# Six slots for expert rows in place of eight, and two more slots for raw weights

## What is computed

```python
def chunk(hc):
    q = (hc @ w_pq).reshape(PEER_CHUNK, PEER_HEADS, 2, PEER_DK_HALF)
    sc = jnp.einsum('thcd,chnd->thcn', q, sub_keys).astype(jnp.float32)
    vals, idx = lax.top_k(sc, PEER_TOPK)
    ...
    experts = jnp.take_along_axis(
    ...
    g = jax.nn.softmax(top_s, axis=-1)
    ue = peer_u[experts]
    ve = peer_v[experts]
    act = jax.nn.gelu(jnp.einsum('td,thkd->thk', hc, ue).astype(jnp.float32), approximate=False)
    return jnp.einsum('thk,thkd->td', (g * act).astype(ve.dtype), ve)
```

## Time and profile before

| what | us |
|---|---|
| median of 3 runs | 1669.24 (1666.39 to 1669.46) |
| the profiled execution | 1668.97 |
| its span | 1667.2 |
| TensorE, VectorE, ScalarE, GpSimd busy | 1503.3, 1122.0, 750.1, 280.2 |
| mean granted TensorE clock | 0.983 of full |

### The profile page before, as it was taken

The page is one execution under the profiler, slowest core; times in us unless marked ns, Lnnn a source line. Parts: engine busy times, 40 slices in busy tenths (PEclk is TensorE's granted clock), DMA queues, the critical chain, the costliest instruction groups (busy, mean ns, idle before and its releaser), DMA issues.

```text
span 1667.2 us, 19514 instructions
## 1 busy us (share of the span) xinstructions
PE 1503.3 (90%) x7240; PEld 1106.9 (66%) x7240; DVE 1122.0 (67%) x2043; ACT 750.1 (45%) x1393; POOL 280.2 (17%) x317
## 2 busy tenths in 40 slices
PE   7999999999688888788898777779999999899999
PEld 6899988988544444344453232248888879788887
DVE  6669656665877676777876866457576656857654
ACT  5544553344344443434543433335555337645532
POOL 0000000000233333334343334312000002000000
PEclk9999999999899999999999999999999999999999
DMA  6744444552799999999999999973455653135553
GB/s 238 266 177 174 156 152 159 195 172 81 286 422 421 420 422 420 421 421 421 414 406 421 410 422 418 421 290 104 170 182 180 199 177 133 51 118 191 195 187 117
DMA packets 71310, 443.07 MB, mean 266 GB/s; under 512 B 7047, under 2 KB 9359, under 8 KB 25776
## 3 DMA queue, kind: packets, MB, share of 16 engines
q0 software_dynamic: 36864, 268.45, 38.8%
q1 hardware_dynamic: 30624, 165.69, 28.7%
q10 hardware_dynamic: 3728, 7.70, 1.3%
HBM read 440.75 MB, written 2.63 MB: 266 GB/s over the span
## 4 chain that ended last, share of the span: by engine, by line
PE 62%; DMA 20%; DVE 12%; ACT 4%; issue 3%; POOL 0%; ACTq 0%; SPq 0%; DVEq 0%; POOLq 0%
DMA arena<-experts,xn 19%; PE banks L1295 18%; PE banks L1326 11%; PE banks L1698 10%; PE banks L1266 9%; PE banks L1331 6%; DVE arena L2293 3%; PE banks L1588 2%; DVE w_lo L1877 2%; PE banks L1424 1%; PE banks L1447 1%; ACT xn L973 1%; ACT xn L977 1%; PE banks L1373 1%; PE banks L1461 1%
## 5 line engine op out<-in xcount | busy, mean ns | idle before, releaser
L1698 PE MATMUL banks<-arena,xn 128*128 128x512 f32 x1024 | 492.7, 618 | 119.6 <-ACT xn L977 119.4
L1877 DVE TENSOR_TENSOR w_lo<-raw,w_hi 128x2048 fp32r<-128x2048 f32 x154 | 352.5, 2290 | 191.0 <-PE banks L1295 94.3
L2293 DVE CUSTOM_DVE_ANT_0 arena<-arena,banks 128x1024 f32<-128x1024 f32 x256 | 311.7, 1218 | 194.0 <-DMA arena<-experts,xn 193.7
L1698 PEld LDWEIGHTS banks<-arena,xn 128*128 128x128 f32 x1024 | 186.2, 195 | 353.1 <-ACT xn L977 184.6
L694 ACT ACTIVATE w_hi<-raw 128x2048 fp32r<-128x2048 f32 x154 | 295.1, 1917 | 255.6 <-PE banks L1295 114.8
L629 POOL DMA_INDIRECT arena<-experts,xn x256 | 247.4, 966 | 425.6 <-PE banks L1698 406.9
L1295 PE MATMUL banks<-w_hi,op 128*128 128x512 f32 x896 | 226.6, 392 | 0.8 <-DVE op L2450 0.8
L966 ACT ACTIVATE xn<-xn,stat 128x2 f32<-128x2 f32 x128 | 37.8, 295 | 379.4 <-DVE xn L2293 379.3
L1326 PE MATMUL banks<-op,w_hi 128*128 128x512 f32 x792 | 199.0, 392 | 0.0
L1295 PEld LDWEIGHTS banks<-w_hi,op 128*128 128x128 f32 x896 | 167.8, 188 | 36.5 <-DVE op L2450 1.3
L1326 PEld LDWEIGHTS banks<-op,w_hi 128*128 128x128 f32 x792 | 142.3, 189 | 26.3 <-issue 1.1
(11 more groups left out here) (254 smaller groups left out, 1363.7 us busy)
## 6 DMA issues: line engine op xcount, KB each, us to landing
raw<-wstream SPq DMA_DIRECT2D x154, 1024.0 KB, 5.1
arena<-experts,xn POOLq DMA_INDIRECT x256, 12.8
xn<-mem_in ACTq DMA_DIRECT2D x2, 1024.0 KB, 7.1
scratch<-scratch ACTq DMA_DIRECT2D x1, 1536.0 KB
x<-x_in SPq DMA_DIRECT2D x2, 512.0 KB, 4.9
arena<-scratch ACTq DMA_DIRECT2D x1, 1024.0 KB, 7.2
raw<-keys_in SPq DMA_DIRECT2D x1, 1024.0 KB, 5.2
raw<-mem_in SPq DMA_DIRECT2D x1, 1024.0 KB, 11.4
```

The costliest lines, as they stand in the source:

```text
L1698: mm = pe.matmul(sums[:, n, :], diag[:, s, :], rows[:, s, D + n * CW:D + (n + 1) * CW], start=(at == 0), stop=(at == PAIRS - 1), skip_grou ...
L1877: dve.tensor_tensor(w_lo[:, n % LO, :, :], raw[:, SLOT[n], :, :], w_hi[:, n % HI, :, :].bitcast(F32), ALU.subtract).then_inc(lo_ready, 1)
L2293: dve.tensor_tensor_reduce(u, u, token_rows[k // PAIRS][:, :, :], 1.0, 0.0, ALU.mult, ALU.add, dots[:, s:s + 1]).then_inc(dot_ready, 1)
```

## The change

`GSLOTS` goes from 8 to 6 and `EXTRA` = 2 is new. `rows` takes the first 6 x 2048 numbers of the arena per partition, and the 4096 behind them become `extra`, two raw slots (3 and 4) for weight halves. Between halves 60 and 71 `ring()` deals the halves out over four slots (two of raw, two extra) in place of two, so that a half waits for the low part of the one four before it. The first half in each extra slot waits for `merged_lo` to be 4 in its stead, since the arena's part is in use by the mixer until then. The wait ahead of half 73 still names the last gather, which now lies in another slot. `diag` keeps its 128 columns per slot, in a view that isn't cut by GSLOTS. Nothing that is computed changes.

```diff
--- before.py
+++ after.py
@@ -42,7 +42,8 @@
 RAW = 3
 HI = 3
 LO = 2
-GSLOTS = 8
+GSLOTS = 6
+EXTRA = 2
 AHEAD = 2
 EXP_AT = 12
 
@@ -93,13 +94,14 @@
 def ring():
 
     first, later = 2 * CHUNKS.index("pq"), 2 * CHUNKS.index("ina")
+    inside = [(SPARE + 1) % RAW, (SPARE + 2) % RAW] + list(range(RAW, RAW + EXTRA))
     slot, turn, before = [], [], []
-    uses, held = [0] * RAW, [None] * RAW
+    uses, held = [0] * (RAW + EXTRA), [None] * (RAW + EXTRA)
     for n in range(NHALF):
         if n == first:
             uses[SPARE] += 2
             held[SPARE] = None
-        s = n % RAW if n < first else (SPARE + 1 + (n - first) % 2) % RAW if n < later else (SPARE + n - later) % RAW
+        s = n % RAW if n < first else inside[(n - first) % len(inside)] if n < later else (SPARE + n - later) % RAW
         slot.append(s)
         turn.append(uses[s])
         before.append(held[s])
@@ -311,6 +313,11 @@
         sub_root = part(6400, S)[0:HEADS, :]
         sub_step = part(6656, S)[0:HEADS, :]
 
+        extra = part(2 * GSLOTS * D, EXTRA, KC, HW)
+
+        def slot_of(n):
+            return raw[:, SLOT[n], :, :] if SLOT[n] < RAW else extra[:, SLOT[n] - RAW, :, :]
+
         keys = raw[:, SPARE, :, :].rearrange("p a (b k) -> p (a b) k", b=2)
         rows = part(0, GSLOTS, 2 * D)
         score = part(16384, TB, 2 * PH, NKEYS)
@@ -362,7 +369,7 @@
         mem_sq, mem_root = spare[:, 0:4, :], spare[:, 4:8, :]
         memory_banks = 4, 5
 
-        diag = xn[:, 0, :].rearrange("p (s n) -> p s n", s=GSLOTS)
+        diag = xn[:, 0, :].rearrange("p (s n) -> p s n", n=P)
         expert = xn[:, 1, 0:256].rearrange("p (t n) -> p t n", t=TB).bitcast(I32)
         weight = xn[:, 1, 256:512].rearrange("p (t n) -> p t n", t=TB)
         dots = xn[:, 1, 784:792]
@@ -379,7 +386,7 @@
         banks = [bank_pairs[i // 2][:, i % 2, :] for i in range(8)]
 
 
-        raw_in = [sem(f"raw_in{i}") for i in range(RAW)]
+        raw_in = [sem(f"raw_in{i}") for i in range(RAW + EXTRA)]
         hi_ready = sem("hi_ready")
         lo_ready = sem("lo_ready")
         norm_hi = sem("norm_hi")
@@ -565,7 +572,7 @@
         @block.sync
         def _(sp):
             def load(n):
-                r, landed = raw[:, SLOT[n], :, :], raw_in[SLOT[n]]
+                r, landed = slot_of(n), raw_in[SLOT[n]]
                 if CHUNKS[n // 2] in WIDE:
                     at = n % 2 * 4 * HW
                     sp.dma_start(r.rearrange("p (b a) c -> p b (a c)", b=2),
@@ -588,12 +595,15 @@
                 if n == 2 * CHUNKS.index("mkvb"):
                     misc_emptied(sp, ("sc", PH - 1))
                     sp.dma_start(mem_rows, mem2_in.rearrange("(t p) d -> p t d", p=P)).then_inc(raw_in[SPARE], 16)
+                if SLOT[n] >= RAW and BEFORE[n] is None:
+                    sp.wait_ge(merged_lo, 4)
                 if BEFORE[n] is not None:
                     sp.wait_ge(lo_ready, BEFORE[n] + 1)
                 if n == 2 * CHUNKS.index("ina"):
                     point(sp, "kmem_b")
                 if n == 2 * CHUNKS.index("ina") + 1:
-                    sp.wait_ge(gathered[GSLOTS - 1], 16 * (TB * PAIRS // GSLOTS))
+                    last = TB * PAIRS - 1
+                    sp.wait_ge(gathered[last % GSLOTS], 16 * (last // GSLOTS + 1))
                 load(n)
 
             for j in range(4):
@@ -691,7 +701,7 @@
 
                     if n >= HI:
                         act.wait_ge(half_done, n - HI + 1)
-                    act.activation(w_hi[:, n % HI, :, :], raw[:, SLOT[n], :, :], ACT.Copy).then_inc(hi_ready, 1)
+                    act.activation(w_hi[:, n % HI, :, :], slot_of(n), ACT.Copy).then_inc(hi_ready, 1)
                 halves[0] = max(halves[0], upto)
 
             def product(key):
@@ -1874,7 +1884,7 @@
 
                     if n >= LO:
                         dve.wait_ge(half_done, n - LO + 1)
-                    dve.tensor_tensor(w_lo[:, n % LO, :, :], raw[:, SLOT[n], :, :],
+                    dve.tensor_tensor(w_lo[:, n % LO, :, :], slot_of(n),
                                       w_hi[:, n % HI, :, :].bitcast(F32), ALU.subtract).then_inc(lo_ready, 1)
                 halves[0] = max(halves[0], upto)
 
```

## The result

The changed kernel takes 1702.15 us (median, 1700.5 to 1706.83), the kernel before 1669.35 in the same measurement: a ratio of **1.0205 (95% interval 1.0193 to 1.0217), slower by some 33 us**. The forecast was 1671.0 with a range up to 1679.0. The profiled execution took 1706.83 us (span 1705.0, mean granted clock of TensorE 0.973), against 1668.97 before; it has the same number of instructions, and most lines of the code stand ten further down (L629 is L639 now, L1698 is L1708, L2293 is L2303).

A forecast was written before the change was run, and what follows sets the result against it. The saturated DMA in the expert stage was taken to bound the kernel. Two halves leaving it gave -4.96 us and five dry stretches with six slots +6.7, net +1.7: about 1671 us, range 1663.8 to 1679.

The forecast's parts named there:

- What bounds the kernel: Expert stage: the 16 DMA engines are saturated for about 667 us, each MB moved costing 2.48 us.
- Two halves leave the stage, -4.96 us: Loads of weight halves 64 and 65 move ahead of the full expert stage, gaining 2 x 2.48 us.
- Least latency 5.8 us: Gathers: shortest issue to landing, taken from the first one on an idle DMA; median was to fall to about 8.
- Rival A: Expert stage: six-slot gathers take longer than 5.8 us, so short stretches cost more; 1677.6 us at 7.0; chance 0.26.
- The fill, 1.7 us: Stretch 453 to 469 us, start of the gathers: six slots leave the DMA engines dry for 1.7 us.
- 469 to 791: Long stretch of the expert stage, in us: smallest issue to landing 11.1, so 0.3 us to spare and no cost.
- m - 4.96 - 5.8: Time to spare with six slots in a stretch whose smallest issue to landing is m; below zero, engines run dry.
- A spell costs its worst row, not the sum: Dry stretches of the expert stage: later rows are already shifted, so each is charged once; five summed to +6.7 us.
- 927 to 950, 2.8 us for the two reciprocals: Expert stage: two 3.35 us VectorE reciprocals hold up dots and slots, so a row lands 2.8 us late.
- The quiet cadence and the tail: Stage end: a pair of gathers every 4.97 us, and unchanged time behind the last landing.
- Rival C: Early halves held by a wait taken for met, or VectorE's gate counts: cost without gain, +6.7, 1675.7 us; chance 0.03.
- rival B: Dry spells in the expert stage are free because engines don't end together, so all 4.96 us stay: 1664; chance 0.18.

The follow-up runs named there:

- e6: Kernel before with eight slots, halves 62 and 63 landing early in row slots 6 and 7, and rows weighed one at a time: 1663.74 us, ratio 0.9968.
- e1: Kernel before with GSLOTS 6 in place of 8 and nothing else, no weights in the arena: 1704.5 us, ratio 1.0209.
- e4: Changed kernel, six slots, with ScalarE weighing each row alone in place of in pairs: 1669.32 us, ratio 1.0001.
- e8: Changed kernel with TensorE multiplying only the first 512 of 1024 value columns for most rows, the rest left out: 1679.0 us, ratio 1.0061.
- e7: Kernel before with five slots and rows weighed one at a time: 1708.0 us, ratio 1.0235.
- e15: Kernel before, eight slots, with ScalarE weighing four rows at once in place of two: 1730.38 us, ratio 1.0385.
- e14: Changed kernel with one eighth of low parts 64 to 71, 12 of 48 matmuls per product half and evenly spread gate dots together: 1686.4 us, ratio 1.0111.
- e9b: Changed kernel with VectorE making only one eighth of the low parts of halves 64 to 71, the rest left out: 1701.04 us, ratio 1.0196.
- e10b: Changed kernel with 12 of the 48 matmuls of each product half in the stage, the others left out: 1695.97 us, ratio 1.0166.
- e11: Changed kernel with VectorE's 16 gate dots of a turn spread evenly over its 22 top-16 steps: 1703.62 us, ratio 1.0195.
- e3: Kernel before with seven slots, the small columns beside the rows keeping rings of eight: 1672.66 us, ratio 1.0023.

## Why the prediction was wrong, point by point

- **What bounds the kernel: right for before.** It was the DMA at 421 GB/s, and e6, which moves two halves ahead of the stage and keeps 418 GB/s in it, is faster.
- **Two halves leave the stage, -4.96 us: right in place and time** (404.78 and 417.6; share 0.59 from 400 to 420), and worth it only while the queue is full. With six slots in pairs they bring nothing that can be told from zero: e1 without them takes 1704.5, the changed kernel 1702.15, and the intervals overlap.
- **Least latency 5.8 us: right** (5.4 to 5.6 measured), and so was the median of about 8 (8.1). Rival A's point of decision, 6.1, was not reached, and yet its side came true. By the Trainium skill (page "DMA: Bandwidth & Descriptors", section "Latency and other measured facts") the memory's access time goes from 0.2 us on average to 2 us at high load. The least issue to landing doesn't show it: with the DMA nearly full it was no longer than the 5.8 us of the lone first gather.
- **The fill, 1.7 us: too small.** 2.9 us by bytes from 450 to 460 and 1.0 more to 470 (380 GB/s for 422), as the rejected estimate of 2 to 4 had it.
- **469 to 791, "0.3 to spare. Nothing.": this is the step that failed.** 421 GB/s became 383 from 500 to 600 and 382 from 600 to 700 (100 x 38 / 421 = 9 us each), and 401 from 700 to 800 (5 us). Two errors made it nothing. First, m - 4.96 - 5.8 was read from a kernel in which the queue is full, where the landing time shows only how long the row queued; the least of it doesn't show how far a row can fall behind when, for want of a queue, TensorE idles, gets the lower clock and holds the row 1.8 us longer (3.78 against 1.98). Nor does it show that product turns at 2.67 us a row can't catch up with a DMA at 2.48. The sum over the slot's round, 1.8 us left over, would have told that one such row uses it up. That sum was at hand in the earlier trace rows.
- **"A spell costs its worst row, not the sum": wrong.** It holds where all that follows is shifted alike. But a hole in the issues comes back one round later as a hole in the releases (6.42 us ahead of row 16, 6.96 ahead of row 22), and is only closed by what is left over in a round. Between 450 and 1140 us the number of packets in progress falls below 14 for 0.3 us or more some 30 times (before: 7, those behind the stage's end included), not five times. Rival A had the sentence for it ("If that long stretch ran short each time that TensorE's steps with weights come between the rows it would be worse still") and no number.
- **927 to 950, 2.8 us for the two reciprocals: about right.** The line of the earlier trace rows is the read-out of a dot, 0.08 us; the reciprocal starts in the same moment, and the reading of 3.35 us is right:

```profile
925.51 3.35 DVE L2322 RECIPROCAL raw<-raw 128x512 f32<-128x512 f32 x1
```

  In the changed kernel the two start at 954.5 and 961.6 us, and GpSimd stands 6.41 us without a slot ahead of 965.11. From 955 to 980 us the DMA moves 374 GB/s, where the kernel before has 417 from 900 to 1000: 2.6 us. Much more was lost where nothing had been put down.
- **That the DMA engines either are full or run dry: too coarse.** More than half of the 42 us doesn't show as idle time but as 27 us of extra busy time of queue 0 for the same bytes.
- **The quiet cadence and the tail: right.** From the last landing to the end of the span are 563.4 us, before 562.3. At the end of the stage of the changed kernel, 4.96 and 4.95 us a pair, as in the earlier trace rows:

```profile
1116.06 0.95 POOL L639 DMA_INDIRECT arena<-experts,xn  x1 [2.30 <-PE banks L1708]
...
1121.02 0.94 POOL L639 DMA_INDIRECT arena<-experts,xn  x1 [2.30 <-PE banks L1708]
...
1125.97 0.94 POOL L639 DMA_INDIRECT arena<-experts,xn  x1 [2.29 <-PE banks L1708]
```

  Where nothing holds a slot, six in pairs do keep the DMA full. That is why the quiet end, on which the sum leaned, showed nothing of the loss.
- **Rival C**, that the change doesn't do what it says, fell with SyncE's rows; **rival B** with the result.

**What is shown and what isn't.** Shown: the loss comes from six slots (e1), goes when a slot is held a shorter time (e4, e8) and comes back with fewer slots or a longer hold (e7, e15). Shown too: product turns and the holds of VectorE together make about half of it (e14, with those parts of the work left out); what each is worth alone stays within the intervals of e9b, e10b and e11. Argued from rows alone: that the rest is holes of other origin (the fill, a weight half that moves between two rows of a pair) and their return one round later, kept up by TensorE's lower clock after an idle time. e8 fits, since at half clock its half row holds a slot no longer than a whole row at full clock; no run kept the clock up with all else equal, so this stays open.

## What to carry over

Before slots are taken from a ring in front of a saturated DMA, add up one slot's round (issue to landing on an idle queue, landing to release with the neighbours that it waits for, the issuer's delay) and compare it with slots x service time: here 4 us left over cost 4 to 6 us in all, 1.8 us cost some 35. By the rows, a hole comes back one round later, and anything that is slower than the bottleneck for a few items (a row at half clock, a turn at 2.67 us, 1 MB of weights between two rows) opens it or keeps it open. If memory is wanted, first shorten the time for which a slot is held: with rows weighed singly, six slots took the time of the eight in pairs (e4), and with all eight it made the early loads pay (e6). Don't read a saturated engine's share alone; read GB/s beside it.

## What the runs showed of the hardware

- A gather queue with few requests moves fewer bytes in the same busy time: 398 GB/s per unit of share (390 / 0.98) in the changed kernel against 414 (418 / 1.01) before, and 673 against 647 us of engine time for 268.45 MB. In the record of single packets the 8 KB ones take 0.31 us in both, but 3.5% of the changed kernel's between 450 and 1142 us take over 0.45 us, before 0.4%. What these take above 0.31 us sums to 32 us of the 16 engines' time, before 4, which is the difference. Why they take longer no run shows.
- Some three requests on their way kept most of the rate. Counted from issue to landing, 5.0 were out on average from 500 to 1000 us in the kernel before and 3.05 in the changed one. Not every run has all landings, so for the others the packets have to serve, taken in order, 128 to a gather: 3.6 out before, 3.0 in e4 and e3, and 2.6 in the changed kernel and 2.5 in e7, which lose over 30 us. The number alone doesn't set the loss: e15 has 2.7 and loses 64 us.
- TensorE's idle time costs twice: after 4 to 8 us without work the next row's four matmuls took 3.78 us in place of 1.88 to 1.98.
- A weight load of 1 MB that SyncE sent out 1.0 us behind the start of a gather of 1 MB (whose issue took GpSimd 1.79 us) landed first, 4.9 us after its issue, at 472.7 us, and the gather 8.4 us after its own, at 475.2. The four gathers before it took 5.4 to 5.6.
